# One hybrid attention and expert-lookup layer: modulation rows, an earlier turn of two head tiles, products of the identity, and one gather per tile

## What is computed

```python
ada = c @ w_ada + b_ada                      # 6 pieces of 1024: shift1, scale1, gate1, shift2, scale2, gate2
h = rms_norm(x, norm1_g) * (1 + scale1) + shift1
z = h @ w_in                                 # 1184 columns: SWA queries, keys, values, MLA latents
out_a = swa_mixer(...)                       # 8 heads of 64, window of 2 chunks of 64, distance bias, sink
q = rope(rms_norm(c_q) @ w_uq); k, v = rope/split(rms_norm(c_kv) @ w_ukv)
q = rms_norm(q, q_norm) * 96 ** -0.5;  k = rms_norm(k, k_norm)      # MLA: 8 heads of 96
out_b = softmax(q k^T, causal by chunks) v
x = x + gate1 * (concat(out_a, out_b) @ w_out)
h2 = rms_norm(x, norm2_g) * (1 + scale2) + shift2
# PEER: 8 heads x top 16 of 128 x 128 experts, by two sets of 128 sub-keys
a = gelu(u_table[e] . h2);  y = sum(g * a * v_table[e])
x = x + gate2 * y
```

## Time and profile before

| | |
|---|---|
| median of 3 executions | 1495.8 us (1495.46 to 1496.79) |
| the profiled execution | 1498.02 us, of which the span shown by the profile is 1496.2 us |
| PE busy | 1416.0 us, 95% of the span |
| PEld busy | 1309.5 us, 88% |
| DVE busy | 1223.2 us, 82% |
| ACT busy | 707.6 us, 47% |
| POOL busy | 740.8 us, 50% |
| HBM over the span | 292 GB/s |

### The profile page before, as it was taken

The page is one execution under the profiler, slowest core; times in us unless marked ns, Lnnn a source line. Parts: engine busy times, 40 slices in busy tenths (PEclk is TensorE's granted clock), DMA queues, the critical chain, the costliest instruction groups (busy, mean ns, idle before and its releaser), DMA issues.

```text
span 1496.2 us, 23503 instructions
## 1 busy us (share of the span) xinstructions
PE 1416.0 (95%) x8439; PEld 1309.5 (88%) x8439; DVE 1223.2 (82%) x2649; ACT 707.6 (47%) x1311; POOL 740.8 (50%) x472
## 2 busy tenths in 40 slices
PE   3899899989897999989999999899999999999999
PEld 2564566768897999989999998899999999999998
DVE  3867667865779988958898886569999999999997
ACT  2234546332542688448853883343344334443342
POOL 2001000020467878768777776855555555565540
PEclk9999559999998999999999999999999999999999
DMA  8740100263569999999999999989999999999996
GB/s 319 278 147 1 57 1 1 80 234 137 189 224 333 319 330 334 358 380 321 325 345 402 329 332 351 412 288 372 391 396 386 395 392 391 389 393 392 391 390 228
DMA packets 158259, 438.88 MB, mean 293 GB/s; under 512 B 16768, under 2 KB 50880, under 8 KB 156992
## 3 DMA queue, kind: packets, MB, share of 16 engines
q1 hardware_dynamic: 91488, 244.55, 45.4%
q0 software_dynamic: 46080, 167.79, 29.4%
q10 hardware_dynamic: 20576, 25.05, 4.7%
HBM read 390.11 MB, written 47.22 MB: 292 GB/s over the span
## 4 chain that ended last, share of the span: by engine, by line
PE 75%; DVE 11%; DMA 5%; POOL 5%; ACT 2%; issue 2%; ACTq 0%; SPq 0%; DVEq 0%; POOLq 0%
PE ps L1196 11%; PE ps L1197 11%; PE ps L1198 11%; PE ps L1145 6%; PE ps L1146 6%; PE ps L1147 6%; PE ps L1156 5%; PE ps L915 4%; POOL lo L539 3%; PE ps L1032 2%; DMA raw<-in_u_tiles 2%; PE ps L1002 2%; PE ps L1015 2%; PE ps L1005 1%; POOL row_res L552 1%
## 5 line engine op out<-in xcount | busy, mean ns | idle before, releaser
L779 ACT ACTIVATE hi<-raw 128x1024 fp32r<-128x1024 f32 x256 | 271.2, 1060 | 312.0 <-PE ps L1198 221.7
L539 POOL TENSOR_TENSOR lo<-raw,hi 128x1024 fp32r<-128x1024 f32 x122 | 294.3, 2418 | 146.7 <-ACT hi L779 139.8
L1145 PE MATMUL ps<-h2hi,hi 128*128 128x352 f32 x1024 | 340.2, 332 | 26.2 <-POOL lo L539 17.2
L1146 PE MATMUL ps<-h2lo,hi 128*128 128x352 f32 x1024 | 334.8, 327 | 0.0
L1147 PE MATMUL ps<-h2hi,lo 128*128 128x352 f32 x1024 | 334.3, 327 | 0.0
L1197 PE MATMUL ps<-clo,hi 128*128 128x352 f32 x1008 | 324.1, 322 | 0.0
L1196 PE MATMUL ps<-chi,hi 128*128 128x352 f32 x1008 | 324.1, 322 | 0.0
L1198 PE MATMUL ps<-chi,lo 128*128 128x352 f32 x1008 | 324.1, 322 | 0.0
L1145 PEld LDWEIGHTS ps<-h2hi,hi 128*128 128x128 f32 x1024 | 196.4, 192 | 30.0 <-POOL lo L539 19.2
L552 POOL DMA_INDIRECT row_res<-in_v_tiles,E x91 | 149.9, 1647 | 137.3 <-DVE y_tok L1651 105.8
L1147 PEld LDWEIGHTS ps<-h2hi,lo 128*128 128x128 f32 x1024 | 196.2, 192 | 0.0
(11 more groups left out here) (286 smaller groups left out, 2216.2 us busy)
## 6 DMA issues: line engine op xcount, KB each, us to landing
raw<-in_u_tiles SPq DMA_DIRECT2D x128, 512.0 KB
raw<-in_v_tiles SPq DMA_DIRECT2D x128, 512.0 KB
gelus<-act_out ACTq DMA_DIRECT2D x128, 176.0 KB
act_in<-gelus SPq DMA_DIRECT2D x128, 176.0 KB
gates<-stage SPq DMA_DIRECT2D x32, 512.0 KB
gate<-gates SPq DMA_DIRECT2D x32, 512.0 KB
late<-in_w_ada SPq DMA_DIRECT2D x4, 2048.0 KB, 8.5
qkT<-in_w_ada SPq DMA_DIRECT2D x3, 2048.0 KB, 14.3
```

What stands on the lines that cost most here:

```text
L539: nc.gpsimd.tensor_tensor(lo[m % 3][:], raw[m % 3][:], hi[m % 3][:].bitcast(F32), ALU.subtract).then_inc(u_lo, 1)
L779: nc.scalar.activation(hi[m % 3][:], raw[m % 3][:], ACT.Copy).then_inc(t_hi, 1)
L1145: nc.tensor.matmul(out, hi[n % 3][:, cols], dense(h2hi, k), start=(k == 0), stop=False)
L1146: nc.tensor.matmul(out, hi[n % 3][:, cols], dense(h2lo, k), start=False, stop=False)
```

## The change

It has these parts.

1. Chunks 3 and 1 are "direct" now, and a direct chunk is made as a row: one column of `c` (128 x 1) is the stationary operand and the chunk streams by, 8 products of 512 columns (`modulation_row`). ScalarE copies the 1 x 512 row out of PSUM, and four products of one row by one number turn it into columns (`modulation_turned`). Scale1 is used when chunks 2 and 3 are there; shift1 is waited for only before ScalarE's first addition.
2. The MLA gain goes into ScalarE's copy of the turned queries (a scale per partition), not into a VectorE pass (L1364, four times, falls away). Its load is 96 x 2 numbers, not two broadcasts.
3. `turn_heads(1)` and its copies come before the last z tile; the scores of units 0 and 1 come between the last turns.
4. `keep_busy(n)` issues n transposes of the identity into an unused part of a PSUM bank: 4 + 8 + 6 + 4 between the turns, and 6 in each of the units 0 to 3, 46 in all.
5. Three one-column activations stand ahead of the first Sqrt, of the second Sqrt and of the first Gelu, which moves the loads of their function tables.
6. The key scores of tile 3 get a buffer of their own.
7. GpSimd issues at most one gather per tile before tile 28, and at most three from there on.
8. The Gelu of the gathered rows comes one tile later, and three small VectorE operations for pieces 2 and 4 of the modulation move from ahead of the units to behind them.

The diff, cut to its core:

```diff
-        direct = [ada_order[1]]
+        direct = [ada_order[1], ada_order[3]]
...
-                while g < 2 * SU and (row_step[g - NROWS] <= m - 2 if g >= NROWS else m >= S0 + 3 + g):
+                most = g + (1 if m < build_at[1] else 3)
+                while g < min(2 * SU, most) and (row_step[g - NROWS] <= m - 2 if g >= NROWS else m >= S0 + 3 + g):
                     gather(g)
                     g += 1
...
+            act.wait_ge(eps_ready, 1)
+            nc.scalar.activation(spent[:, 0:1], eps[:], ACT.Sqrt)
...
             nc.scalar.activation(rstd1, ps[:, 6, :], ACT.Sqrt, bias=eps[:], scale=1.0 / D).then_inc(sd1, 1)
+            for j in direct:
+                act.wait_ge(ada_row, direct.index(j) + 1)
+                nc.scalar.activation(ada_rows(j), row_ps(j), ACT.Copy).then_inc(ada_row_sb, 1)
+            act.wait_ge(shift_ready, 1)
...
             copy_projections(3)
+            copy_heads(1)
             square_heads(2)
             root_heads(2)
             copy_z(0, 3)
             square_queries(3)
             square_heads(3)
-            copy_heads(1)
-            for tt in range(3):
+            for tt in range(2):
                 copy_queries(tt)
             root_queries(3)
             root_heads(3)
+            copy_queries(2)
             copy_heads(2)
...
-                if p == 3:
-                    act.wait_ge(s_out[1], 16)
-                to = s if p == 0 else sout[p % 2]
+                to = s if p == 0 else sout[p]
...
-                if n == more_at:
+                if n == more_at + 1:
                     act.wait_ge(row_used, SU)
...
+            def modulation_row(j):
                 n = place["ada", j]
                 arrived(n)
+                for k in range(KD):
+                    last = nc.tensor.matmul(row_ps(j), cT[:, k:k + 1], chunk(n)[:, k, :], start=(k == 0), stop=(k == KD - 1))
+                last.then_inc(ada_row, 1)
+
+            def modulation_turned(j):
+                pe.wait_ge(ada_row_sb, direct.index(j) + 1)
                 for q in range(CH // P):
                     col = j * (CH // P) + q
+                    last = nc.tensor.matmul(ada_at(col), ada_rows(j)[:, q * P:(q + 1) * P], ones[0:1, 0:1],
+                                            start=True, stop=True)
                 last.then_inc(ada_done, 1)
...
-            modulation(ada_order[0])
             pe.wait_ge(sq1_sum, KD - 1)
             nc.tensor.matmul(ps[:, 6, :], ones[:], rstd1, start=True, stop=True).then_inc(ms1, 1)
-            modulation_direct(ada_order[1])
+            modulation_row(ada_order[1])
+            modulation(ada_order[0])
+            modulation_turned(ada_order[1])
+            modulation_row(ada_order[3])
             modulation(ada_order[2])
-            modulation(ada_order[3])
+            modulation_turned(ada_order[3])
...
+            def keep_busy(count):
+                for _ in range(count):
+                    nc.tensor.transpose(ps[:, 7, P:2 * P], ident[:], ident[:])
...
+            for tt in range(3):
+                turn_queries(tt)
+            keep_busy(4)
+            turn_heads(2)
             scores(0)
             scores(1)
+            keep_busy(8)
+            turn_queries(3)
+            keep_busy(6)
+            turn_heads(3)
+            keep_busy(4)
             for u in range(NU):
                 if u + 2 < NU:
                     scores(u + 2)
+                if u < 4:
+                    keep_busy(6)
                 transposes(u)
...
-            for j in prepared[1:3]:
-                modulate(j)
+            modulate(prepared[1])
             dve.wait_ge(small_in, 16 * NSMALL)
-            modulation(1, 4)
+            modulation(1, 2)
...
-            modulation(0, 4)
             for k in range(KD):
                 nc.vector.scalar_tensor_tensor(out=hT[:, k, :], in0=res[:, k, :], scalar=gs[:, k:k + 1], in1=rstd1,
                                                op0=ALU.mult, op1=ALU.mult).then_inc(h_scaled, 1)
+                if k == 5:
+                    modulation(0, 4)
+                    dve.sem_inc(shift_ready, 1)
```

More of the change, by code:

```diff
@@ L82, in region @@
             return out, at
-        (res, ident, ones, iota, cT, b_cols, ada, g1, g2, gs, eps), at0 = region(BASE, [
+        (res, ident, ones, iota, cT, b_cols, ada, g1, g2, gs, eps, spent), at0 = region(BASE, [
             ("res", [P, KD, T], F32),
@@ L201, in build @@
         ms1 = sem("ms1")
+        eps_ready = sem("eps_ready")
         sd1 = sem("sd1")
@@ L325, in acc, with ada_at, row_ps, ada_rows @@
             return (accs_late if j in (6, 7, 10, 11) else accs)[:, prepared.index(j) % 2, :]
+        def ada_at(col):
+            return ps[:, 3, col:col + 1] if col < KD else ada_ps[:, col:col + 1]
+        def row_ps(j):
+            return ps[0:1, 4 + direct.index(j), :]
+        def ada_rows(j):
+            at = T * (1 + direct.index(j))
+            return pb[:].rearrange("p a j k -> p (a j k)")[0:1, at:at + CH]
         def chunk(n):
@@ L755, in _ @@
             high_w(("out", 1))
+            nc.scalar.activation(spent[:, 1:2], eps[:], ACT.Sqrt)
             for k in range(KD):
@@ L768, in _ @@
             high_w(("query", 1))
+            nc.scalar.activation(spent[:, 2:3], eps[:], ACT.Gelu)
             for h in range(PH):
@@ L841, in _ @@
                     gelu(n)
+                    if i == 0 and p == 1:
+                        act.wait_ge(s_out[1], 32)
                     if i == 0 and p >= 2:
@@ L873, in modulation @@
                     col = j * (CH // P) + q
[L874 removed]
+                    last = nc.tensor.matmul(ada_at(col), acc(j)[:, q * P:(q + 1) * P],
                                             ones[:, 0:1], start=True, stop=True)
                 last.then_inc(ada_done, 1)
[L878 removed]
+            def modulation_row(j):
                 n = place["ada", j]
                 arrived(n)
+                for k in range(KD):
[3 more added lines that the diff above has]
+                pe.wait_ge(ada_row_sb, direct.index(j) + 1)
                 for q in range(CH // P):
                     col = j * (CH // P) + q
[L884 to L886 removed]
+                    last = nc.tensor.matmul(ada_at(col), ada_rows(j)[:, q * P:(q + 1) * P], ones[0:1, 0:1],
+                                            start=True, stop=True)
                 last.then_inc(ada_done, 1)
[L888 to L889 removed]
+                pe.sem_inc(chunk_used[slot[place["ada", j]][0]], 1)
             pe.sem_inc(oh_used, 2)
@@ L979, in _ @@
             project(3)
+            turn_heads(1)
             z_tile(0, 3)
-            turn_heads(1)
-            for tt in range(3):
-                turn_queries(tt)
-            turn_heads(2)
-            turn_queries(3)
-            turn_heads(3)
-            pe.wait_ge(mt_sb, 4 * TT)
-            pe.wait_ge(zq_sb, TT)
             def scores(u):
                 kind, b, sub, j0 = units[u]
+                if u == 0:
+                    pe.wait_ge(zq_sb, 2)
                 if u >= 3:
@@ L1252, in modulation @@
                 cols = slice(piece * KD, (piece + 1) * KD)
-                settled(tt_(ada[:, cols], ada_ps[:, cols], b_cols[:, cols], ALU.add))
+                settled(tt_(ada[:, cols], ps[:, 3, cols] if piece == 0 else ada_ps[:, cols], b_cols[:, cols], ALU.add))
             dve.wait_ge(c_in, 16)
@@ L1305, in _ @@
                 settled(nc.vector.memset(distm[0:64, b, 192:256], MASKED))
-            for j in prepared[3:7]:
+            for j in prepared[2:6]:
                 modulate(j)
@@ L1432, in copy_out @@
                 ins.then_inc(o_sb, 1)
-            for piece in (2, 4):
-                modulation(piece, 8)
-            settled(nc.vector.scalar_tensor_tensor(out=gs[:], in0=ada[:, 4 * KD:5 * KD], scalar=1.0, in1=g2[:],
-                                                   op0=ALU.add, op1=ALU.mult))
             bias_and_max(0)
@@ L1450, in low_w @@
                 tt_(wlo[:], chunk(place[key]), whi[:].bitcast(F32), ALU.subtract).then_inc(w_split, 1)
+            for piece in (2, 4):
+                modulation(piece, 8)
+            settled(nc.vector.scalar_tensor_tensor(out=gs[:], in0=ada[:, 4 * KD:5 * KD], scalar=1.0, in1=g2[:],
+                                                   op0=ALU.add, op1=ALU.mult))
             for k in range(KD):
```

42 lines of the change are left out of this document (20 added, 22 removed).

## The result

The changed kernel took 1504.9 us (median of 5 runs, 1502.6 to 1510.2), the kernel before 1495.6 in the same comparison: ratio 1.0064, 95% interval 1.0043 to 1.0084. It is 0.6% slower; I had forecast 1474. The profiled execution took 1502.6 us, span 1500.8.

A forecast was written before the change was run, and what follows sets the result against it. TensorE, 95% busy, was taken as the bound, at half clock from 150 to 224 us. The terms -6.5 + 2 - 17.1 - 2.6 + 1.5 + 0.5 + 0.2 = -22.0 gave 1474 us, range 1460 to 1493.

The forecast's parts named there:

- Start, -6.5: Start: modulation rows run fast, z tiles begin at 47.3 instead of 51.74 us, first z tile runs fast throughout; -6.5 us.
- heads: Turns of the heads: added identity products outweigh the VectorE passes saved; +2 us, bounds -1 and +5.
- Units, -17.1: "s" units: at full clock VectorE becomes the bound, the 12 steps take 30.0 instead of 47.1 us; -17.1 us.
- rival 3: Units stay at half clock: identity products don't hold it over waits, or "s" units lose it; +3.1, 1499 us, chance 0.12.
- Key scores, -2.6: Expert part: ScalarE's wait for the store of the first keys goes away; -2.6 us, bounds 0 and -2.7.
- Gathers, +1.5: Expert part: the stall behind tile 20 moves to tile 28, with a clock dip behind it; +1.5 us, bounds 0 and +3.
- Both go away, 11.1 us: Behind tile 20: TensorE's 8.4 us wait for the gather burst and the next dot product's extra 2.7 us both vanish.
- The rows come in time: Gather k, issued with tile 14 + k at 442.6 + 3.84 k us, lands 5.5 us later, before VectorE's use.
- rival 5: Rows late: one gather per tile starves the search, TensorE waits 5 to 15 us more at tile 28; about 1484 us, chance 0.05.
- Gelu one tile later and the rest: Gelu later: VectorE waits 3.8 us more, +0.5 (bounds 0 and +3); table loads 0; moved additions +0.2.

The follow-up runs named there:

- e4: The kernel before with only the limit on gathers (one to a tile before the first build, three after): 1501.5 us, ratio 1.0044.
- e1: The changed kernel without its 46 products of the identity: 1499.0 us, ratio 1.0023 to the kernel before.
- e11: e10 with 20 products of the identity instead of 4 ahead of turn_heads(2): 1471.9 us, ratio 0.9865 to the kernel before.
- e5: The changed kernel with 18 identity products instead of 6 ahead of the first turned probabilities, none in later units: 1481.5 us, ratio 0.9917 to the kernel before.
- e12: The kernel before with 18 products of the identity added behind scores(2), ahead of the first turned probabilities: 1477.5 us, ratio 0.9872.
- e9: e5 with row gathers two to a tile from tile 13 instead of one from tile 14: 1474.3 us, ratio 0.9873 to the kernel before.
- e10: e9 with the key scores' read-back for the second and third search four tiles later: 1474.9 us, ratio 0.9864 to the kernel before.
- e8: The kernel before with the key scores' read-back for the second and third search four tiles later: 1494.4 us, ratio 0.9992.
- e6: The changed kernel with 6 identity products in each of the 16 "s" units, the wait left unfilled: 1492.4 us, ratio 0.9971 to the kernel before.
- e2: The changed kernel with the gathers of before (up to eight behind one tile): 1497.8 us, ratio 0.9989 to the kernel before.

## Why the prediction was wrong

Three differences of ratios divide up the +9.6 us. Limit on gathers alone (e4): +0.44%, 6.6 us. The 46 products (after against e1): +0.41%, 6.1 us. All the rest of the change (e1 against e4, which both have the limit): -0.21%, -3.1 us, give or take as much. That they add up to 0.64% is so by construction and checks nothing. The forecast of -22 failed in two steps: the units, where -17.1 us did not come because the clock was lost ahead of them, and the gathers. By the prediction's steps:

**Start, -6.5.** The mechanism was right: the row is fast, 8.87 and 7.03 us (forecast 9.0 and 6.9). Over all 14 traces (the kernel before, the changed one and the twelve experiments) the z tiles begin at 44.9 to 46.1 us with the new order and 51.2 to 51.7 with the old. But I carried this gain through to the heads, and half is lost by then: the last z copy comes at 141.2 to 143.5 against 144.6 to 146.1, and the first exponentials (e11 with its filled gap aside) at 158.1 to 161.5 against 160.4 to 164.3. Start and heads together gave some 2 us, not 4.5. The trace of the kernel before, from which I worked, has the latest first exponentials of the four traces that share its program up to there. Where between 50 and 140 us the other 3 us go was not tried.

**Units, -17.1.** This step failed as the prediction made it. It asked whether 2.05 busy of 2.5 us in a unit holds the clock (e5: it does) and whether the identity products of the first four units are free (they are not, at half clock). It did not ask whether the products cover the wait ahead of the units: TensorE waits some 2.3 us for the first exponentials, the change's six products fill 0.88 of it and 1.40 stay empty. The clock fell there, in the changed kernel's trace; 18 products (2.18 us) hold it in that of e5. In the old kernel it falls one wait earlier, and 18 products at the same place bring it back (e12). The size was right: the 12 steps take 28.4 us in e5 (163.27 to 191.63), where the forecast was 30.0 and before it was 47.1. In time, e12 is 1.3% faster than before (19 us) and e5 1.06% faster than e1 (16 us). So rival 3 came about, at the place of its first clause, "they do not hold it over the waits", and its second clause, that the "s" units lose the clock, is refuted by the trace of e5. By the mean clock, 5 of the 24 executions of e5, e9, e10 and e11 lost it somewhere with the wait filled; where and why is not shown.

Of the rule of the Trainium skill ("TensorE: Matmul & The Clock Gate", Part 4) that transposes don't engage the full clock, e12's trace disagrees once more: its clock rose from half to full under 18 transposes that stood behind 6 score products.

**Key scores, -2.6.** The wait of the earlier trace rows went, but the load behind it landed no sooner and that wait grew from 3.49 to 6.00 us; the clock fell behind TensorE's wait of 2.37 us, and -2.2 at dot 0 became +2.0 at dot 6. So in this trace the term is at best 0. No experiment isolates it: in e1, from the same kernel, the lead goes only from 6.7 us at dot 0 to 5.4 at dot 6.

**Gathers, +1.5.** The stall moved to dot 28 as forecast, and the cold dot behind it came too. But it cost 6.6 us (e4), outside my 0 to +3. Two sentences failed. "Both go away, 11.1 us": a wait of 4.9 us stayed behind dot 19 (5.7 in e4). By the traces there are two causes, SyncE's wait of 10.3 us in front of the tiles' loads and GpSimd's burst. e4 and the changed kernel take the second away, e8 the first (8.0 us stay), and neither removes the wait. That the two together are all of it is not shown: in e10, which has neither, gathers two to a tile made a wait of 4.3 us of another kind. "The rows come in time": I had reckoned gathers at an even 3.84 us, but a gather goes behind its tile's remainder, and where the tiles stall, the rows stall. In e4 VectorE stands 5.61 + 2.18 = 7.8 us for them, near the 6.6 us that it cost. The burst had happened to feed VectorE through that stall. This is rival 5 (rows late), together with rival 3.

**Gelu one tile later and the rest.** VectorE waits 3.7 us more, as forecast; what it costs in time was not isolated.

What is open: half of the start's gain, the executions that lose the clock although the wait is filled, what a filler at the earlier wait of the old kernel would do, and why the time lost at dot 28 is partly made up by dot 61 (+7.1 to +3.7).

## What to carry to other kernels

Before asking whether a stretch of work holds the clock, look at the last wait ahead of it: here a stretch of "s" units with no filler in it kept the level that it was entered with, half or full. A filler that covered the wait wholly was worth 16 to 19 us (e5 against e1, e12 against before), and 46 products that left 1.40 us of it empty cost 6 us. And look where the clock falls before you say which wait does it: in the old kernel it was not the last one. Before spreading a burst in a queue, list what else stands in the queues at that place (here SyncE's wait for a buffer), and what the burst's data feeds meanwhile. A stall with two causes in two queues need not answer to the removal of one (e4, e8).

## What the runs showed of the hardware

- In the "s" units at half clock TensorE was fully busy for 47 us, and the clock stayed at 0.50 (before, 168 to 216 us); with six transposes in each it rose near 180 us (e6); and once at full clock it stayed there with TensorE 4.04 of 5.00 us busy (e5, 165 to 170 us).
- When the "m" units begin earlier at half clock, the rise does not come earlier by as much. From the first "m" score to the last it is 209.9 to 265.5 us (e1, 55.6 us), 216.0 to 269.2 (before, 53.2 us), and at full clock 191.6 to 245.1 (e5, 53.5 us).
- The mean granted clock differs between executions of one program, and the time with it: in e2, with 1.40 us of the wait empty, 2 of 12 took 1478.1 us at 0.985 and the others 1496.2 to 1501.8 at 0.967 to 0.969; in e9, with the wait filled, five took 1472.1 to 1475.8 us at 0.987 or 0.988, and one 1492.7 at 0.974.
- A matrix product with one stationary column took no less and no more than one with 128: 8 of them (16 records) with 512 streamed columns in 7.03 us, and 7.11 us for 16 records of z products with the same 512 columns.
